# Fifteen blocks of the experts' first layer worked out during the scatter of a PEER layer, read from a turned table, in place of twelve turned on TensorE

## What is computed

```python
u = jnp.take(expert_u, idx_blk, axis=0)
act = jax.nn.gelu(jnp.einsum('thkd,td->thk', u, h_blk))
vv = jnp.take(expert_v, idx_blk, axis=0)
return jnp.einsum('thk,thkd->td', g_blk * act, vv)
```

## Time and profile before

| | us |
|---|---|
| median of the runs (2) | 2916.08 |
| lowest, highest | 2914.36, 2917.8 |
| the profiled execution, its own time | 2919.07 |
| its span, first to last instruction | 2917.3 |
| PE busy | 2822.0 (97%) |
| DVE busy | 2409.6 (83%) |
| ACT busy | 1118.3 (38%) |
| POOL busy | 1229.4 (42%) |

### The profile page before, as it was taken

One profiled execution on the slowest core, in us unless ns is written; L12 is line 12 of the kernel. 1 busy time (PEld: TensorE's weight loads), 2 busy tenths in 40 slices (PEclk: granted clock), 3 DMA queues, 4 the chain that ended last, 5 costly groups with the idle time before them and its releaser, 6 DMA issues.

```text
span 2917.3 us, 48123 instructions
## 1 busy us (share of the span) xinstructions
PE 2822.0 (97%) x16232; PEld 2504.0 (86%) x16232; DVE 2409.6 (83%) x4564; ACT 1118.3 (38%) x2211; POOL 1229.4 (42%) x990
## 2 busy tenths in 40 slices
PE   6999999999999999999999999999999999999997
PEld 4888888888788899988888898898888888888896
DVE  6345666675689989979999989889998999999898
ACT  7221555523356656643333332323332333332233
POOL 0001000010178830026666556556565556655553
PEclk9999999999999999999999999999999999999998
DMA  7427444234311129899999999999999999999999
GB/s 280 160 86 240 111 118 119 97 134 153 137 43 52 63 97 279 271 342 376 358 358 373 367 344 346 342 339 360 370 358 348 353 370 354 371 358 354 356 365 280
DMA packets 335309, 771.65 MB, mean 265 GB/s; under 512 B 22048, under 2 KB 161344, under 8 KB 329160
## 3 DMA queue, kind: packets, MB, share of 16 engines
q0 software_dynamic: 117296, 423.15, 38.7%
q1 hardware_dynamic: 210168, 342.87, 34.9%
q10 hardware_dynamic: 7712, 3.93, 0.4%
HBM read 692.95 MB, written 76.92 MB: 264 GB/s over the span
## 4 chain that ended last, share of the span: by engine, by line
PE 44%; DVE 13%; DMA 7%; issue 5%; DVEq 2%; POOL 1%; ACT 1%; POOLq 0%; ACTq 0%; SPq 0%
PE psum L2610 17%; PE psum L2603 16%; PE psum L203 6%; DMA ex_v_row<-in_expert_v,ex_row 4%; PE psum L1717 3%; DVE ex_u_row L2859 3%; DVE acc L2871 3%; DVE sc_hg L2273 2%; DVEq L2272 1%; DVE sc_hi L2267 1%; DMA w_dram<-sc_w 1%; PE psum L1902 1%; DMA ex_u_row<-in_expert_u,ex_row 1%; DVE sc_hj L2264 1%; DVE ex_v_lo L2854 1%
## 5 line engine op out<-in xcount | busy, mean ns | idle before, releaser
L2561 POOL DMA_INDIRECT ex_u_row<-in_expert_u,ex_row x384 | 416.9, 1086 | 714.7 <-DVE ex_dot L2859 390.5
L2561 POOL DMA_INDIRECT ex_v_row<-in_expert_v,ex_row x384 | 533.2, 1388 | 167.8 <-issue 108.5
L2871 DVE SCALAR_TENSOR_TENSOR acc<-ex_v_row,ex_coef,acc 128x1024 f32<-128x1024 f32 x381 | 488.4, 1282 | 56.3 <-DMA ex_v_row<-in_expert_v,ex_row 55.6
L2859 DVE CUSTOM_DVE_ANT_0 ex_u_row<-ex_u_row,h_rows 128x1024 f32<-128x1024 f32 x384 | 466.0, 1214 | 6.2 <-DMA ex_u_row<-in_expert_u,ex_row 5.7
L2610 PE MATMUL psum<-ex_v_hi,ex_c_lo 128*128 128x512 f32 x1260 | 342.2, 393 | 14.2 <-DVE ex_v_lo L2854 13.7
L2610 PE MATMUL psum<-ex_v_lo,ex_c_hi 128*128 128x512 f32 x1260 | 338.8, 391 | 0.0
L2610 PE MATMUL psum<-ex_v_hi,ex_c_hi 128*128 128x512 f32 x1260 | 338.4, 391 | 0.0
L2610 PEld LDWEIGHTS psum<-ex_v_hi,ex_c_lo 128*128 128x128 f32 x1260 | 234.7, 189 | 64.4 <-issue 18.0
L2603 PE MATMUL psum<-h_hi,h_lo 128*128 128x320 f32 x1648 | 278.2, 311 | 11.7 <-DVE acc L2933 8.7
L2610 PEld LDWEIGHTS psum<-ex_v_lo,ex_c_hi 128*128 128x128 f32 x1260 | 237.5, 188 | 50.3
L2610 PEld LDWEIGHTS psum<-ex_v_hi,ex_c_hi 128*128 128x128 f32 x1260 | 237.7, 189 | 50.0
(11 more groups left out here) (368 smaller groups left out, 5321.2 us busy)
## 6 DMA issues: line engine op xcount, KB each, us to landing
ex_vn<-in_expert_v SPq DMA_DIRECT2D x64, 1024.0 KB, 7.2
ex_w<-w_dram SPq DMA_DIRECT2D x64, 640.0 KB, 10.3
ex_un<-in_expert_u_t SPq DMA_DIRECT2D x39, 1024.0 KB, 8.6
w_dram<-sc_w SPq DMA_DIRECT2D x9, 4096.0 KB, 15.2
gm_wm<-in_w_mod_rest SPq DMA_DIRECT2D x28, 512.0 KB, 6.2
ex_un<-in_expert_u_t SPq DMA_DIRECT2D x25, 512.0 KB, 7.7
pj_raw<-in_w_in SPq DMA_DIRECT2D x11, 1024.0 KB, 7.2
pr_wm<-in_w_mod_first SPq DMA_DIRECT2D x8, 1024.0 KB, 14.5
```

The source lines that it names most:

```text
L2561: nc.gpsimd.indirect_dma_start(to[:], None, all_rows, bass.IndirectOffsetOnAxis(row[s][:, col:col + 1], 0)).then_inc(done, 16)
L2859: nc.vector.tensor_tensor_reduce(out=u_row[k % 3][:], in0=u_row[k % 3][:], in1=h_rows[:, k % 3, :], scale=1.0, scalar=0.0, op0=ALU.mult, o ...
L2871: nc.vector.scalar_tensor_tensor(out=to, in0=v_row[k % 3][:], scalar=coef[:, k:k + 1], in1=to, op0=ALU.mult, op1=ALU.add).then_inc(row_use ...
```

## The change

The jobs' blocks now come from `expert_u_t`, a copy of the table in DRAM in which the width is already in the partitions (the retrieval's 13 blocks and the experts use it already). TensorE's `turn` and `leave` go, and so does the constant `minus`. ScalarE makes the upper part straight from the loaded tile in one operation of 1024 columns, and VectorE the lower part in one subtraction of 1024 columns (`lower`, as the experts' `split_u` does). A job takes two groups in place of three: a half is hidden behind each of the groups 0 to 29, and `EXTRA` goes from 9 to 12, so 15 jobs in place of 12, `LATE` from 6 to 3, and three periods more of the experts hide 12 halves in place of 14. ScalarE's upper part of job k+1 stands ahead of the evictions of group 2k, VectorE's lower part behind its work for group 2k+1. SyncE loads job k+2 in group 2k, ahead of the store of job k's first half.

```diff
-    EXTRA = 9
+    EXTRA = 12
...
     def load(self, sp, n, m):
-        sp.wait_ge(self.turned, (n - self.HEADS) * 2 + 2)
-        sp.dma_start(self.un[m][:], self.u_rows[:, bass.ds(self.block(n), 1), :].rearrange("j a d -> j (a d)")).then_inc(self.un_in[m], 16)
+        sp.wait_ge(self.lowered, n - 1)
+        self.fetch(sp, n, self.un[m])
...
+        sp.dma_start(to[:].rearrange("p k x -> p (k x)"), self.u_columns[step, :, e, :]).then_inc(loaded, 16)
...
     def hide(self, pe, n, m, half):
-        if n < self.HEADS:
-            pe.wait_ge(self.lowered, n + 1)
-        else:
-            pe.wait_ge(self.lo_out, (n - self.HEADS) * 2 + 4)
+        pe.wait_ge(self.lowered, n + 1)
...
+        act.wait_ge(*self.rows_in(n - self.HEADS))
+        act.wait_ge(self.hidden, n * 2 + 2)
+        self.nc.scalar.activation(self.ut_hi[m], self.un[m][:], ACT.Copy).then_inc(self.raised, 1)
+
+    def lower(self, dve, n, m):
+
+        dve.wait_ge(self.raised, n + 1)
+        self.nc.vector.tensor_tensor(self.ut_lo[m], self.un[m][:], self.ut_hi[m].bitcast(F32), ALU.subtract).then_inc(self.lowered, 1)
...
         @block.tensor
         def _(pe):
-            ahead.turn(pe, *self.job(0))
...
     def vector(self, dve, then):
...
+            if g == 0:
+                self.ahead.lower(dve, *self.job(0))
+            elif g % 2 and g // 2 + 1 < self.JOBS:
+                self.ahead.lower(dve, *self.job(g // 2 + 1))
...
     def tensor(self, pe, then):
...
                 last.then_inc(self.copied, 1)
-            k = g // 3
-            if k < self.JOBS and g % 3 < 2:
-                ahead.hide(pe, *self.job(k), g % 3)
-            if k + 1 < self.JOBS and g % 3 >= 1:
-                n, m = self.job(k + 1)
-                if g % 3 == 1:
-                    ahead.turn(pe, n, m)
-                else:
-                    ahead.leave(pe, n, m)
+            if g // 2 < self.JOBS:
+                ahead.hide(pe, *self.job(g // 2), g % 2)
...
     def scalar(self, act, then, between):
...
+            if g % 2 == 0 and g // 2 + 1 < self.JOBS:
+                ahead.upper(act, *self.job(g // 2 + 1))
...
     def sync(self, sp, then):
...
-        for k in range(1, 3):
-            ahead.load(sp, *self.job(k))
+        ahead.load(sp, *self.job(1))
         for g in range(self.GROUPS):
-            tile, k = g // self.NG, g // 3
-            if k < self.JOBS and g % 3 < 2:
-                ahead.store(sp, self.job(k)[0], g % 3)
-            if k + 3 < self.JOBS and g % 3 == 1:
-                ahead.load(sp, *self.job(k + 3))
+            tile, k = g // self.NG, g // 2
+            if k + 2 < self.JOBS and g % 2 == 0:
+                ahead.load(sp, *self.job(k + 2))
+            if k < self.JOBS:
+                ahead.store(sp, self.job(k)[0], g % 2)
```

More of the change, by code:

```diff
@@ L1684, in store @@
         sp.dma_start(self.dram[bass.ds(n, 1), :, half, :].rearrange("a e t -> e (a t)"), self.g[half][:]).then_inc(self.stored[half], 16)
[L1686 to L1700, removed]
-            self.nc.tensor.matmul(self.turn_bank[q].rearrange("p (k n) -> p k n", k=4), self.t.minus[:], self.ut(self.ut_hi, m, q),
-                                  start=False, stop=True, skip_group_check=True).then_inc(self.left, 1)
     def hide(self, pe, n, m, half):
-        if n < self.HEADS:
-            pe.wait_ge(self.lowered, n + 1)
-        else:
-            pe.wait_ge(self.lo_out, (n - self.HEADS) * 2 + 4)
+        pe.wait_ge(self.lowered, n + 1)
         pe.wait_ge(self.gelued, n * 2 + (half + 1))
@@ L1997, in _ @@
         chunk(0)
-        nc.scalar.activation(t.minus[:], t.ident[:], ACT.Copy, scale=-1.0)
         chunk(1)
@@ L2231, in _ @@
             nc.scalar.activation(self.gp[0][:], left("gate"), ACT.Copy, scale=self.GATE_SCALE).then_inc(self.rounded, 1)
-            ahead.lower(act, *self.job(0))
             for g in range(GATHERED):
@@ L2279, in tensor @@
         nc, ahead = self.nc, self.ahead
-        ahead.leave(pe, *self.job(0))
         for g in range(self.GROUPS):
@@ L2316, in scalar @@
                                           scale=1.0 / self.GATE_SCALE).then_inc(self.evicted, 1)
-            k = g // 3
-            if k < self.JOBS and g % 3 < 2:
-                ahead.gelu(act, self.job(k)[0], g % 3)
-            if k + 1 < self.JOBS and g % 3 >= 1:
-                (ahead.upper if g % 3 == 1 else ahead.lower)(act, *self.job(k + 1))
+            if g // 2 < self.JOBS:
+                ahead.gelu(act, self.job(g // 2)[0], g % 2)
             if g == self.GROUPS - 1:
@@ L2439, in periods @@
     def periods(eng, first, last):
-        for start, end, is_late in ((first, LATE, False), (LATE, last, True)):
+        for start, end, is_late in ((first, LATE, False), (LATE, last, True)) if first < LATE else ((LATE, last, True),):
             late[0] = is_late
```

36 lines of the change are left out of this document (10 added, 26 removed).

## The result

| | us |
|---|---|
| before, median of the runs (2) | 2916.08 |
| changed, median of the runs (2) | 2948.0 (2944.43, 2951.57) |
| ratio | 1.0109, 95% interval 1.0093 to 1.0125 |
| the profiled execution of the changed kernel, its own time and its span | 2951.57, 2949.6 |

The changed kernel is 32 us slower, 1.1%: within the 2% but plainly slower. I had forecast +16, range 2910 to 2946. The measured median lies 2 us above the top of that range, so the forecast failed, in size and not in sign.

The account below looks back on a forecast made before the run. PE was taken to bound the experts, DVE by a hair the scatter, with both full there. Terms -0.9 + 18.4 + 17.4 + 2 - 21 gave about +16, median 2932 us; own range 2922 to 2942, 8-in-10 range 2910 to 2946.

Parts of the forecast that it names:

- The start: Scatter's start: without PE's turn of job 0, the transposes of the picks begin earlier, -0.9 us.
- The pace: Scatter: PE sets 5.42 us a group in groups 0 to 29, DVE 4.705 in 30 to 39; stage +18.4 us.
- The loads: Scatter: six job loads wait behind a tile's store in SP's queue, each stopping PE 2.9 us, +17.4 us.
- The rival by which the loads come in time: Scatter: loads behind a tile's store land early enough, so no stops; -3.5 us, 2912.6; chance 0.20.
- the second: Another name for The rival with stops of full length.
- The rival with stops of full length: Scatter: PE hides none of each 6.1 us wait and each stop brings the low clock; +43, 2959; chance 0.08.
- The clock: Scatter: PE's clock may drop to 1.2 GHz after the six stops and in light groups; +2 us, bounds 0 to 10.
- The experts: Experts: three periods go from 14 halves to 12, about 6.9 us shorter each; -21 us taken.
- The rival by which the experts give nothing: Experts: DMA engines, not PE, set the period, so three periods stay at 105 us; +37, 2953; chance 0.04.

Follow-up runs that it names:

- experiment 1: The changed kernel with each job's load issued one group earlier, ahead of the gelu store and the tile's store: 2920.56 us, ratio 1.0013.
- experiment 2: The changed kernel with EXTRA 9 in place of 12, so 12 jobs as before the change, loads left as in the change: 2946.77 us, ratio 1.0110.
- experiment 9: experiment 1 with half blocks in five of every six groups up to group 34, in place of each of groups 0 to 29: 2917.43 us, ratio 1.0001.

## Why the prediction failed, step by step

*The start* (-0.9): -3.0 in the profile. Among the kernels here the first eviction lies between 1071.3 and 1076.3, so what the missing turn saves can't be read better than that.

*The pace* (+18.4): +19.9 in experiment 1, where nothing else is added. Right, and half blocks 5.42 apart as forecast (gelus at 1101.97 and 1107.40).

*The loads* (6 x 2.9 = 17.4): 17.5 in six stops, by the mechanism forecast: store, load behind it, ACT's upper part, evictions, PE. That the totals agree to 0.1 us is partly luck: single stops lie between 2.41 and 3.99. The rival by which the loads come in time had nothing behind it: none of the six did. What I wrote of completion out of order belongs to this rival too, not to the second as I put it; all six loads landed 1.2 to 2.2 us behind their tile's store. The rival with stops of full length overrated them, since PE's half block hid half of each wait.

*The clock* (+2): too small. Scatter minus pace minus stops is 44.7 - 19.9 - 17.5 = 7.3, and by the cycles above 6.2 of it is the low clock behind three stops. The price of 1.7 us for 3.4 us of low clock was right; how often it would come was not. I had 0 to 10 as bounds from the earlier trace rows, and chose near the bottom because no row showed a single stop of 3 us doing it. Three of six did, the first for 6.8 us. In experiment 2 two of four did, again at 1.7 us each by its cycles. By the page "TensorE: Matmul & The Clock Gate" of the Trainium skill, section "HAM oscillation — how this bites in real kernels", which I weighed, the total would have been 2940; the trace now agrees in three of six stops.

*The experts* (-21, bounds -20.7 to -22.3): the step that failed most. They gave 9.3 in the changed kernel, 15.1 in experiment 1. I priced a light period by two that stood among light ones, 6 and 7, and multiplied by three. The bounds were far too narrow: they came from the length of the periods removed, never from what the new ones would meet. The trace before already had it. V's split, its rows of step 35 and period 8's end, then of step 53 and period 13:

```profile
2200.43 1.92 ACT L2707 ACTIVATE ex_v_hi<-ex_vn 128x2048 fp32r<-128x2048 f32 x1 [8.01 <-PE psum L2610]
2229.00 1.90 ACT L2707 ACTIVATE ex_v_hi<-ex_vn 128x2048 fp32r<-128x2048 f32 x1
...
2621.40 1.90 ACT L2707 ACTIVATE ex_v_hi<-ex_vn 128x2048 fp32r<-128x2048 f32 x1
...
2647.81 1.92 ACT L2707 ACTIVATE ex_v_hi<-ex_vn 128x2048 fp32r<-128x2048 f32 x1 [7.96 <-PE psum L2610]
2676.00 1.90 ACT L2707 ACTIVATE ex_v_hi<-ex_vn 128x2048 fp32r<-128x2048 f32 x1
...
2724.52 1.90 ACT L2707 ACTIVATE ex_v_hi<-ex_vn 128x2048 fp32r<-128x2048 f32 x1
```

Step 35 takes 28.6 us and step 53 28.2, and the light periods 8 and 13 take 104.1 and 103.1 in place of 98. These steps are 18 apart, and 18 ahead of step 35 lies step 17, in period 4. With 104 for period 4 and 98 for 3 and 5 the term is about -16, where experiment 1 gave -15.1: the third block takes away the slack ahead of step 17 and is worth nothing (+1.5 with its scatter). In the changed kernel period 3 has a second slow step besides (26.4 us, 22.9 in experiment 1), and period 1 takes 3.8 us more than there. These lie behind most of the 5.7 us between the two profiles; no run tells where they come from, and only 2 to 3 us of them stand in the medians (27.4 apart, of which the scatter is 24.8), so part can be the execution that was profiled. The rival by which the experts give nothing was wrong in its reason (periods 3 to 5 did get shorter, by 12.1 us in all), but nearer in its price than I allowed.

The sum of the misses in the profile: -2.1 (start), +1.6 (pace and stops), +5.3 (clock and rest), +11.7 (experts), so +16.5 on the 15.9 forecast, 32.4.

## What to carry to other kernels

Read a transfer's latency by what stands ahead of it in its own queue: a load that is due soon goes ahead of a large store or into another engine's queue, and moving one entry of the stream does it. When work is moved off the busiest engine, count what the new form gives the second busiest in total over the stage, for a stage in balance can get longer by nearly the whole of that (here 16.0 us for 17.0 of added work, experiment 9). And a repeated saving need not be worth the same each time: price it from the place where the next unit goes, look through the whole trace for a stall that comes round (here every 18 steps), and expect a unit to be worth little where it takes away the slack that hid it.

## What I had not expected of the hardware

SP can be held by an issue while the transfers ahead of it drain: for 11.22 us by a load of 512 KB behind 4 MB [the row at 1097.87], until 3 us before the 4 MB had landed, and for 6.8 us by a gelu store in the middle of it (experiment 1, at 1101.94). A subtraction on GpSimd lengthens the operation of VectorE beside it from 1.22 to 3.44 us. Of ten stops of PE behind a late load (six in the changed kernel, four in experiment 2), five brought 1.2 GHz: those of 2.45, 2.63, 3.39, 3.99 and 4.59 us; those of 2.40, 2.41, 2.44, 2.54 and 2.87 us did not.
